# Differential attention: part of the weights' lower halves made by GpSimd, four of eight heads turned by blocks through memory

## The reference, cut to what matters

```python
def diff_attn_mixer(h, pos, w_in, ...):
    q, k, v = split_cols(h @ w_in, [D_MODEL, D_MODEL, D_MODEL])
    q = rms_norm(q.reshape(bsz, seq, nh, 2, dh), g_q)      # nh = 8, dh = 64
    k = rms_norm(k.reshape(bsz, seq, nh, 2, dh), g_k)
    q, k = rope(q), rope(k)
    s = jnp.einsum('bhtqd,bhtkd->bhtqk', q_blk, kt) * scale  # t = 0, 1: two maps for a head
    pr = jax.nn.softmax(s, axis=-1)
    a = pr[:, :, 0] - lam * pr[:, :, 1]
    o = jnp.einsum('bhqk,bhkd->bhqd', a, vt)
    o = rms_norm(o, g_sub) * (1.0 - lambda_init)
    return o.reshape(bsz, seq, D_MODEL) @ w_out
```

## Time and profile before

| | us |
|---|---|
| median of 3 runs (lowest, highest) | 888.64 (888.57, 890.1) |
| the profiled execution | 889.01 |
| its span in the trace | 887.2 |
| PE busy | 882.0 |
| DVE busy | 673.0 |
| ACT busy | 502.6 |
| POOL busy | 80.3 |

### The profile page before, as it was taken

One profiled execution on the slowest core, in us unless ns is written; L12 is line 12 of the kernel. 1 busy time (PEld: TensorE's weight loads), 2 busy tenths in 40 slices (PEclk: granted clock), 3 DMA queues, 4 the chain that ended last, 5 costly groups with the idle time before them and its releaser, 6 DMA issues.

```text
span 887.2 us, 12026 instructions
## 1 busy us (share of the span) xinstructions
PE 882.0 (99%) x4286; PEld 729.0 (82%) x4286; DVE 673.0 (76%) x1041; ACT 502.6 (57%) x820; POOL 80.3 (9%) x92
## 2 busy tenths in 40 slices
PE   9999999999999999999999999999999999999998
PEld 8988888888888888778888888888888888887777
DVE  6997688666746699997787666645879987779863
ACT  6666464444535576787564444444665445577681
POOL 1002010000000403111100000000010000115300
PEclk9999999999999999999999999999999999999999
DMA  9754568676667566423387666775777774757701
GB/s 341 264 179 177 202 259 304 237 272 243 244 217 241 213 233 242 144 98 117 128 301 261 244 241 239 253 242 179 255 294 256 240 243 158 292 169 244 234 23 48
DMA packets 85315, 194.51 MB, mean 219 GB/s; under 512 B 7300, under 2 KB 38404, under 8 KB 85256
## 3 DMA queue, kind: packets, MB, share of 16 engines
q1 hardware_dynamic: 83544, 189.15, 61.2%
q0 software_dynamic: 1280, 3.93, 1.4%
q10 hardware_dynamic: 432, 0.66, 0.2%
HBM read 175.23 MB, written 18.48 MB: 218 GB/s over the span
## 4 chain that ended last, share of the span: by engine, by line
PE 93%; DVE 5%; issue 1%; DMA 1%; ACT 0%; DVEq 0%; ACTq 0%
PE bank L1871 83%; PE bank L1909 3%; DVE wlo L1134 2%; PE bank L2186 1%; PE bank L2266 1%; PE bank L1924 1%; PE bank L2296 1%; DVE df_m L1552 1%; DVE df_tok L1556 1%; DVE df_stat L1576 1%; DMA h<-x_dram 1%; DVE df_ss L1528 1%; PE bank L2160 0%; PE bank L2252 0%; PE bank L2075 0%
## 5 line engine op out<-in xcount | busy, mean ns | idle before, releaser
L1134 DVE TENSOR_TENSOR wlo<-raw,whi 128x1024 fp32r<-128x1024 f32 x295 | 346.7, 1214 | 30.5 <-ACT whi L723 30.1
L723 ACT ACTIVATE whi<-raw 128x1024 fp32r<-128x1024 f32 x295 | 301.6, 1059 | 111.5 <-PE bank L1871 101.1
L1871 PE MATMUL bank<-whi,x_hi 128*128 128x512 f32 x560 | 152.4, 394 | 0.0
L1871 PE MATMUL bank<-wlo,x_hi 128*128 128x512 f32 x560 | 149.9, 389 | 0.0
L1871 PE MATMUL bank<-whi,x_lo 128*128 128x512 f32 x560 | 149.8, 389 | 0.0
L1871 PEld LDWEIGHTS bank<-wlo,x_hi 128*128 128x128 f32 x560 | 105.1, 188 | 22.2
L1871 PEld LDWEIGHTS bank<-whi,x_lo 128*128 128x128 f32 x560 | 105.1, 188 | 22.0
L1871 PEld LDWEIGHTS bank<-whi,x_hi 128*128 128x128 f32 x560 | 103.6, 188 | 22.7 <-issue 1.8
L1871 PE MATMUL bank<-whi,y_hi 128*128 128x512 f32 x396 | 107.6, 394 | 0.1
L1871 PE MATMUL bank<-whi,y_lo 128*128 128x512 f32 x396 | 106.1, 390 | 0.0
L1871 PE MATMUL bank<-wlo,y_hi 128*128 128x512 f32 x396 | 106.0, 389 | 0.0
(11 more groups left out here) (260 smaller groups left out, 891.9 us busy)
## 6 DMA issues: line engine op xcount, KB each, us to landing
raw<-stream_dram SPq DMA_DIRECT2D x295, 512.0 KB, 4.7
...
mb_blocks<-p_tok POOLq DMA_DIRECT2D x10, 192.0 KB, 3.8
mb_pT<-mb_blocks POOLq DMA_DIRECT2D x10, 192.0 KB, 4.3
...
```

Of the source, the lines that this page charges most:

```text
L723: A(whi[:, u % RING, :], raw[:, u % SLOTS, :], ACT.Copy).then_inc(sem("w_hi"), 1)
L1134: V.tensor_tensor(wlo[:, u % SLOTS, :], raw[:, u % SLOTS, :], whi[:, u % RING, :].bitcast(F32), ALU.subtract).then_inc(sem("w_lo"), 1)
L1871: last = T.matmul(bank[pair + t][:, :], lhs[a][:, kt, t * P:(t + 1) * P], w[:, place(w, u), kk * NW:(kk + 1) * NW], start=part != 1 and k ...
```

## The change: what it does

1. GpSimd makes the lower parts of the eight units in `BY_POOL` (9, 11, 17, 18, 20, 22, 24, 26 of this mixer). DVE skips them, and PE waits for whichever engine's count applies (`lower_of`).
2. Heads 0, 2, 3 and 4 are no longer turned by PE. DVE transposes 32 x 32 blocks (`df_blocks`), POOL issues a write to memory and a read back, and ACT copies the landed map to `df_aT` with the order of blocks changed. The step of ACT keeps its name, aT.
3. The PSUM banks are one tensor, so one reduction takes the maxima of both maps of a head, and one instruction scales them. ACT's exponentials of the first map now wait for the maxima of both.
4. The rotation does both halves of the tokens together, stage by stage.
5. The tables are written anew: on PE the turn of head 1 goes from unit 18 to 19, the qkT step 5 from 19 to 18. On DVE the rotation of tile 3 stands whole before soft 1, and the sums of tile 1 stand before its rotation.

```diff
+DF_TRIPS = (0, 2, 3, 4)
+DF_TURNED = tuple(_h for _h in range(8) if _h not in DF_TRIPS)
...
+BY_POOL = tuple(END[DF_IN] + _u for _u in (9, 11, 17, 18, 20, 22, 24, 26))
...
+        (13, "soft", 0), (13, "blk", 0), (16, "unit", 2), (17, "scores", 2), (17, "rope", 3), (17, "soft", 1), (17, "scores", 3),
+        (0, "split", 9), (2, "split", 11), (4, "sums", 0), (8, "sums", 1), (10, "split", 17), (12, "sums", 2), (12, "split", 18), (13, "split", 20), (13, "out", 0),
+        (14, "split", 22), (14, "in", 0), (15, "split", 24), (16, "sums", 3), (17, "split", 26), (18, "out", 2), (19, "out", 3), (19, "in", 2),
...
+def lower_of(u):
+
+    if u in BY_POOL:
+        return "w_lo_pool", BY_POOL.index(u) + 1
+    return "w_lo", u + 1 - sum(v <= u for v in BY_POOL)
...
-        bank = [ctx.enter_context(nc.psum_tensor(f"bank{b}", [P, NW], F32)) for b in range(8)]
+        psum = ctx.enter_context(nc.psum_tensor("bank", [P, 8, NW], F32))
+        bank = [psum[:, b, :] for b in range(8)]
...
+        aland = sb("df_land", [P, 2, NW], scope=landing)
+        ablk = sb("df_blk", [P, 2, NW], scope=staging)
...
+            def split(u):
+
+                c.wait(pool, "w_hi", u + 1)
+                nc.gpsimd.tensor_tensor(wlo[:, u % SLOTS, :], raw[:, u % SLOTS, :], whi[:, u % RING, :].bitcast(F32),
+                                        ALU.subtract).then_inc(sem("w_lo_pool"), 1)
+
...
+            def df_out(hd):
+
+                n = DF_TRIPS.index(hd)
+                pool.wait_ge(sem("mb_blk"), n + 1)
+                nc.gpsimd.dma_start(a_dram[n], ablk[:, n % 2, :]).then_inc(sem(f"mb_out{n % 2}"), 16)
+
+            def df_in(hd):
+
+                n = DF_TRIPS.index(hd)
+                pool.wait_ge(sem(f"mb_out{n % 2}"), 16 * (n // 2 + 1))
+                if n >= 2:
+                    pool.wait_ge(sem("df_aT"), DF_COPIED.index(DF_TRIPS[n - 2]) + 1)
+                nc.gpsimd.dma_start(aland[:, n % 2, :].rearrange("p (i w) -> p i w", i=P // B),
+                                    a_dram[n].rearrange("q n -> (q n)").rearrange("(i p w) -> p i w", i=P // B, p=P))\
+                    .then_inc(sem(f"mb_land{n % 2}"), 16)
+
...
+            def turned_aside(hd):
+
+                if hd in DF_TRIPS:
+                    act.wait_ge(sem("mb_blk"), DF_TRIPS.index(hd) + 1)
+                else:
+                    act.wait_ge(sem("df_aT_filled"), DF_TURNED.index(hd) + 1)
...
-                    act.wait_ge(sem("df_aT_filled"), DF_P_AFTER[hd] + 1)
+                    turned_aside(DF_P_AFTER[hd])
...
-                    act.wait_ge(sem("df_max"), 4 * hd + 2 * (m + 1))
+                    act.wait_ge(sem("df_max"), 2 * (hd + 1))
...
+                if hd in DF_TRIPS:
+                    n = DF_TRIPS.index(hd)
+                    act.wait_ge(sem(f"mb_land{n % 2}"), 16 * (n // 2 + 1))
+                    A(daT[:, hd % 4, :].rearrange("p (n i b) -> p n i b", n=4, b=B),
+                      aland[:, n % 2, :].rearrange("p (i n b) -> p n i b", n=4, b=B), ACT.Copy).then_inc(sem("df_aT"), 1)
+                    return
+                act.wait_ge(sem("df_aT_filled"), DF_TURNED.index(hd) + 1)
                 A(daT[:, hd % 4, :], bank[6][:, :], ACT.Copy).then_inc(sem("df_aT"), 1)
...
+                    if u in BY_POOL:
+                        continue
...
-            def df_rope(t, k):
+            def df_rope(t):
...
-                for k in (k,):
+                for k in range(TT):
...
+                for k in range(TT):
+                    x3 = dtok[:, t % 2, k, :].rearrange("p (a e) -> p a e", a=4)
                     dve.wait_ge(sem("df_swap"), 2 * (TT * t + k + 1))
-                    V.tensor_tensor(x3, x3, cs, ALU.mult).then_inc(sem("df_cos"), 1)
+                    V.tensor_tensor(x3, x3, rot[:, w, 0, k, :].unsqueeze(1).to_broadcast([P, 4, P]), ALU.mult)\
+                        .then_inc(sem("df_cos"), 1)
+                for k in range(TT):
+                    xt = dtok[:, t % 2, k, :]
                     dve.wait_ge(sem("df_cos"), TT * t + k + 1)
                     V.tensor_tensor(xt, xt, dm2[:, k, :], ALU.add).then_inc(sem("df_rope"), 1)
...
-                for m in range(2):
-                    dve.wait_ge(sem("df_scores"), 2 * hd + m + 1)
-                    V.tensor_reduce(stt[:, 2 * m:2 * m + 2], bank[DF_S_BANKS[hd][m]][:, :].rearrange("p (q k) -> p q k", q=TT),
-                                    AXX, ALU.max).then_inc(sem("df_max"), 1)
-                    dve.wait_ge(sem("df_max"), 4 * hd + 2 * m + 1)
-                    V.scalar_tensor_tensor(stt[:, 4 + 2 * m:6 + 2 * m], stt[:, 2 * m:2 * m + 2], -1.0,
-                                           factors[:, :, hd % 4, m], ALU.mult, ALU.mult).then_inc(sem("df_max"), 1)
+                b = DF_S_BANKS[hd][0]
+                dve.wait_ge(sem("df_scores"), 2 * (hd + 1))
+                V.tensor_reduce(stt[:, 0:4].rearrange("p (m q) -> p m q", m=2),
+                                psum[:, b:b + 2, :].rearrange("p m (q k) -> p m q k", q=TT), AXX, ALU.max)\
+                    .then_inc(sem("df_max"), 1)
+                dve.wait_ge(sem("df_max"), 2 * hd + 1)
+                V.scalar_tensor_tensor(stt[:, 4:8].rearrange("p (m q) -> p m q", m=2),
+                                       stt[:, 0:4].rearrange("p (m q) -> p m q", m=2), -1.0,
+                                       factors[:, hd % 4, :, :], ALU.mult, ALU.mult).then_inc(sem("df_max"), 1)
...
+            def df_blocks(hd):
+
+                n = DF_TRIPS.index(hd)
+                dve.wait_ge(sem("df_a"), TT * (hd + 1))
+                if n >= 2:
+                    dve.wait_ge(sem(f"mb_out{n % 2}"), 16 * (n // 2))
+                for q in range(TT):
+                    last = V.transpose(ablk[:, n % 2, :].rearrange("p (f k q b) -> p q f k b", f=P // B, q=TT, b=B)[:, q],
+                                       DF_P[hd][:, 0, q, :].rearrange("p (k b f) -> p f k b", b=B, f=P // B))
+                last.then_inc(sem("mb_blk"), 1)
...
-                            c.wait(pe, "w_lo", u + 1)
+                            c.wait(pe, *lower_of(u))
...
-                free[6] = ("df_aT", hd + 1)
+                free[6] = ("df_aT", DF_COPIED.index(hd) + 1)
```

More of the change, by code:

```diff
@@ L162 @@
+        (24, "aT", 4), (24, "aT", 5), (25, "aT", 6), (26, "av", 5), (26, "aT", 7), (26, "pair", 1), (27, "av", 7), (28, "pair", 2),
         (28, "pair", 3),),
     "dve": (
-        (5, "rope", 0), (6, "more", 0), (6, "sums", 0), (8, "rope", 1), (8, "sums", 1), (8, "more", 1),
-        (9, "unit", 1), (11, "sums", 2), (11, "rope", 2), (11, "more", 2), (11, "scores", 0), (12, "scores", 1),
-        (13, "soft", 0), (16, "unit", 2), (17, "scores", 2), (17, "soft", 1), (17, "rope", 3), (17, "scores", 3),
@@ L167 @@
-        (17, "sums", 3), (17, "more", 3), (18, "soft", 2), (19, "scores", 4), (19, "soft", 3), (19, "scores", 5),
-        (19, "soft", 4), (21, "scores", 6), (22, "osums", 0), (22, "scores", 7), (22, "norm", 0), (22, "soft", 5),
+        (5, "rope", 0), (6, "sums", 0), (8, "sums", 1), (8, "rope", 1),
+        (9, "unit", 1), (11, "sums", 2), (11, "rope", 2), (11, "scores", 0), (12, "scores", 1),
+        (13, "soft", 0), (13, "blk", 0), (16, "unit", 2), (17, "scores", 2), (17, "rope", 3), (17, "soft", 1), (17, "scores", 3),
@@ L1615, in _ @@
                     head_sums(arg, dsq65, dss, "df_sq", "df_ss", "df_rstd")
[L1616 to L1617 removed]
+                elif step == "rope":
+                    df_rope(arg)
                 elif step == "unit" and arg in (1, 2):
@@ L1626, in _ @@
                     df_soft(arg)
+                elif step == "blk":
+                    df_blocks(arg)
                 elif step == "osums":
```

74 lines of the change are left out of this document (41 added, 33 removed), and 2 rows, old and new, of the table DF_ORDER.

## The result

The changed kernel takes 894.20 us (median of 6 runs, 893.77 to 896.95); the kernel before took 889.37 beside it. The ratio is 1.0064, 95% interval 1.0054 to 1.0073: about 5.7 us slower. (The two medians are 4.8 apart, as three of the six executions before took 890 us or more; in the later batches its median was 888.35 to 888.59.) The forecast was 891.2, with 893.6 as its upper end. The sign was right; the +2.6 of the forecast is less than half of the measured 5.7, and the time lies 0.6 above the range.

A forecast was written before the change was run, and what follows sets the result against it. PE was taken as the bound (busy 882.0 of 887.2 us), VectorE and ACT close behind. The profiled 889.01 plus 2.6 at w_out gave 891.6, less 0.37 for a median 891.2; range 887.0 to 893.6.

The forecast's parts named there:

- +2.6: At the first unit of w_out on PE: start at 409.7 against 407.13, 2.6 us later, added to the profiled time.
- PE's part: On PE: four of eight head turns go, 1.65 us off, all swallowed in the delay before w_out.
- The string behind the scores of head 4: From head 4's scores (388.2) to w_out (409.7): ACT sets the end, its exponentials delayed by VectorE's late maxima.
- VectorE's own sum: VectorE's work without locks: subtractions, joined maxima and rotation save, block transposes add 4.4; 7.4 us lighter in all.
- POOL's subtraction and the lock: A POOL subtraction takes some 2.4 us and locks out VectorE's two-input instructions: 1.5 us lost a piece, 10.5 in all.
- one lock (unit 17) falls where VectorE would wait for squares: On VectorE: the lock by POOL's subtraction of unit 17 falls in a wait for squares, so is of the harmless kind.
- the lock of unit 24: On VectorE: after soft-max 1 ends at 381.4, POOL's subtraction of unit 24 delays maxima 3, scaled at 383.8.
- rival (c): Locks bite twice, unit 24's inside soft-max 1, which ends at 383.5; w_out at 411, +3.9, 892.5 us; chance 0.22 with beyond.
- a wait of 2.2 at the scores of head 4: On PE: scores of head 4 start at 388.2 against 386.03, waiting on ACT's exponentials and copies, +2.2 us.
- No cushion: Head 2's map lands at 400.3 to 401, ACT reaches its copy at 400.1; each us more of landing delays PE.
- rival (b): VectorE relieved, but head 2's map lands late and ACT waits 2.4 us: +0.9 at w_out, 889.5 us; chance 0.27.
- Rival (a): VectorE is really relieved, 7.4 us lighter, and no engine holds PE: 2.3 us faster, 886.3 us; chance 0.15.

The follow-up runs named there:

- e4: Changed kernel with POOL's eight subtractions replaced by a memset of the same place, which reads nothing: 887.97 us, ratio 0.9996 to the kernel before.
- e6: Changed kernel with the lower parts of units 17 and 24 made by VectorE again, six left on GpSimd: 891.69 us, ratio 1.0038 to the kernel before.
- e10: Changed kernel with 14 identity transposes added on PE ahead of head 1's turn, to fill its wait: 893.37 us, ratio 1.0056 to the kernel before.
- e9: The changed kernel itself run once more, nothing changed, for a second profile: 895.37 us, ratio 1.0073 to the kernel before.
- e14: Kernel before with the joined rotation, and VectorE also making blocks of heads 2, 3 and 4 that nobody uses: 890.99 us, ratio 1.0032.
- e1: Changed kernel with all lower parts made by VectorE again, the rest as changed: 891.60 us, ratio 1.0030 to the kernel before.
- e7: Changed kernel with all lower parts by VectorE, blocks of heads 3 and 4 and copies of heads 2 and 3 moved later: 890.66 us, ratio 1.0023.

## Why the prediction was right or wrong

- *PE's part* held: four turns of 0.4 us are gone, and all is swallowed by waits. The string behind the scores of head 4 held too: from these scores of head 4 to `w_out` it has 21.5 us (388.2 to 409.7), the profile 21.46, with the lock of unit 26 on the scaling of maxima 4 as forecast (1.34 for 0.16). All that was missed lies ahead of these scores, which started at 391.04.
- *VectorE's own sum* held. Joined maxima 1.21 + 0.16; a pair of block transposes 1.16 to 1.20 (two of 0.61).
- *POOL's subtraction and the lock* held: 2.40 and 2.49 for the 2.4, 1.6 us lost a piece on the seven (1.8, 2.2, 1.2, 1.6, 0.95, 2.1, 1.2, each the locked row less its like: 11.1 for 10.5). The rule of the Trainium skill (SBUF — State Buffer, "Who interferes with whom") is borne out by both sides: beside POOL's memset, which reads nothing, VectorE's subtractions stayed free (e4), and beside POOL's subtraction VectorE's reductions did.
- **The step that failed first:** "one lock (unit 17) falls where VectorE would wait for squares", taken at nothing. POOL reached it only at 350.73, behind its small powers, and it fell on the rotation of tile 1, for which PE's k tile waits: 2.2 us of VectorE and a wait of 1.76 on PE, gone in e6. I had followed where POOL gets its data, not what stood ahead on POOL's own queue.
- **The second:** the lock of unit 24 was laid on maxima 3 after soft-max 1 had ended at 381.4. It fell inside soft-max 1, which ended at 385.0. Soft-max 0 had ended at 370.9, not 368.1, since relief and locks do not cancel by there; the order at unit 22 gave a part back, and the rotation ended at 381.6, not 380.0. So soft-max 1 came 1.4 us late, and 381.4 + 1.4 + 2.1 from the lock is 384.9. That is rival (c)'s mechanism, 0.22 of the chance, with (c) itself moved by what unit 17 did. And PE waited at the turn of head 1, 2.6 us, where I had a wait of 2.2 at the scores of head 4 (measured 0.25). The forecast named this place as one that would make it wrong.
- **Not in any case:** the half clock behind that wait. It takes 1.5 us from PE, 0.7 to 0.9 at `w_out` by e10. Nor that the order at unit 22 is left to chance (e9), 1.3 to 1.5 us when it goes the other way.
- *The sum:* at `w_out` the forecast had +2.6, the profile has +5.4. The 2.8 between them are there at the scores of head 4: 0.9 is the half clock (5.98 us from the turn for 5.09 in e10), about 1.9 is soft-max 1, late and locked. Rival (c), soft-max 1 at 383.5 and +3.9, had the string behind it dearer than it is: 5.7 us to the scores for 5.15 in e10 (385.19 to 390.34), and 21.8 from there for 21.45. The forecast's own upper end stands once as 892.0 and once as 892.4; the time is above both.
- *Trips:* ACT's copy of head 2 did not wait for its landing in the changed kernel (402.98, without a wait), since all before it was late. "No cushion" was wrong for e4 as well, rival (b)'s case: it forecast 2.4 us of waiting for head 2 and there were 0.1, with 0.70 for head 3. Their price is the blocks on VectorE (e14), and at times the half clock behind the wait that these bring (e1, e7). I counted that work in VectorE's sum but thought the relief beside it would carry it; yet even with the subtractions gone and no lock (e4) the change only came level. Rival (a)'s 886.3 was 1.7 too low for its own case: there ACT's string, late by its waits for maxima (1.67 at head 5) and the landing of head 3, held `w_out` at 406.58 (PE waited 1.17).

Open: how the chance at unit 22 is shared out between executions, how much of the time unit 17 takes and how much unit 24 (only e6 bears on it, with both), and why the clock falls in some executions of e1 and e7 and not in others.
